# Gated delta rule on one core: both runs inverted at once in 64-row halves, and a shorter table of constants

## The reference

```python
gam = jnp.cumsum(gc, axis=-1)
incl = jnp.tril(jnp.ones((CHUNK, CHUNK), bool))
strict = jnp.tril(jnp.ones((CHUNK, CHUNK), bool), -1)
decay = jnp.exp(jnp.where(incl, gam[..., :, None] - gam[..., None, :], -jnp.inf))
kk = jnp.einsum("bhnld,bhnsd->bhnls", kc, kc)
a_mat = jnp.where(strict, bc[..., :, None] * kk * decay, 0.0) + jnp.eye(CHUNK, dtype=q.dtype)
rhs = jnp.concatenate([vc * bc[..., None], kc * (bc * jnp.exp(gam))[..., None]], axis=-1)
sol = lax.linalg.triangular_solve(a_mat, rhs, left_side=True, lower=True, unit_diagonal=True)
u, w = sol[..., :dv], sol[..., dv:]
qk = jnp.einsum("bhnld,bhnsd->bhnls", qc, kc) * decay
q_dec = qc * jnp.exp(gam)[..., None]
k_dec = kc * jnp.exp(gam[..., -1:] - gam)[..., None]
...
    v_new = u_i - jnp.einsum("bhld,bhdv->bhlv", w_i, state)
    o_i = jnp.einsum("bhld,bhdv->bhlv", qd_i, state) + jnp.einsum("bhls,bhsv->bhlv", qk_i, v_new)
    state = cd_i[..., None, None] * state + jnp.einsum("bhld,bhlv->bhdv", kd_i, v_new)
```

## Time and profile before

| | |
|---|---|
| time, median of 3 runs | 3710.27 us (3708.34 to 3712.47) |
| the profiled execution | 3719.07 us, its span 3716.9 us |
| mean granted TensorE clock of the span | 0.919 |
| busy: PE, DVE, ACT, POOL | 3155.8, 1509.2, 884.0, 310.2 us |
| gd_chunks | 2275.97 to 2402.96 us of the span |

### The profile page before, as it was taken

The page is one execution under the profiler, slowest core; times in us unless marked ns, Lnnn a source line. Parts: engine busy times, 40 slices in busy tenths (PEclk is TensorE's granted clock), DMA queues, the critical chain, the costliest instruction groups (busy, mean ns, idle before and its releaser), DMA issues. The chain is left out here.

```text
span 3716.9 us, 94167 instructions
## 1 busy us (share of the span) xinstructions
PE 3155.8 (85%) x41870; PEld 2282.9 (61%) x41870; DVE 1509.2 (41%) x2497; ACT 884.0 (24%) x1486; POOL 310.2 (8%) x259
## 2 busy tenths in 40 slices
PE   4978879998787788886997947775899999999996
PEld 2855467887464666674886936733466666666653
DVE  3353653333653554546565875535111111111111
ACT  2113323222222343331453532201011111010110
POOL 0020200000311122230000014200000000000000
PEclk6988899999897999998998968987899999999998
DMA  5253432222033100103653510030999999999993
GB/s 199 80 161 123 152 135 102 91 101 103 34 129 143 49 21 28 42 4 125 227 198 117 187 64 1 28 140 28 350 405 405 406 406 406 406 407 406 405 406 146
DMA packets 220145, 684.74 MB, mean 184 GB/s; under 512 B 25776, under 2 KB 50608, under 8 KB 187008
## 3 DMA queue, kind: packets, MB, share of 16 engines
q1 hardware_dynamic: 190144, 648.49, 45.7%
q10 hardware_dynamic: 29760, 32.69, 2.6%
HBM read 660.15 MB, written 20.97 MB: 183 GB/s over the span
## 5 line engine op out<-in xcount | busy, mean ns | idle before, releaser
L3358 PE MATMUL experts_psum_gu<-ring,experts_x 128*32 128x256 f32 x9216 | 508.6, 381 | 16.4 <-ACT experts_x L3402 16.4
L3358 PEld LDWEIGHTS experts_psum_gu<-ring,experts_x 128*32 128x32 f32 x9216 | 294.9, 110 | 220.9 <-ACT experts_x L3402 16.9
L3462 DVE TENSOR_TENSOR experts_gate<-experts_psum_gu,experts_bias 128x768 f32<-128x768 f32 x32 | 30.6, 958 | 864.6 <-PE experts_psum_gu L3358 864.6
L3381 PE MATMUL experts_psum_down<-experts_weights,experts_hiddenT 128*32 128x256 f32 x6144 | 338.8, 380 | 3.8 <-ACT experts_hiddenT L3410 3.8
L3381 PEld LDWEIGHTS experts_psum_down<-experts_weights,experts_hiddenT 128*32 128x32 f32 x6144 | 199.4, 110 | 137.3 <-issue 5.5
L811 PE MATMUL mlp_psum_bank<-mlp_x_high,mlp_w_high 128*128 128x512 f32 (+1 forms) x512 | 175.7, 343 | 12.5 <-DVE xT_rounded L328 12.5
L302 DVE TENSOR_TENSOR ring_rounded<-ring,mlp_w_high 128x1024 fp32r<-128x1024 f32 x128 | 156.7, 1226 | 51.0 <-ACT mlp_w_high L297 51.0
L811 PE MATMUL mlp_psum_bank<-xT_rounded,mlp_w_high 128*128 128x512 f32 (+1 forms) x512 | 173.8, 339 | 0.0
L3406 ACT ACTIVATE experts_sigmoid<-experts_gate 128x768 f32<-128x768 f32 x32 | 27.0, 843 | 616.1 <-DVE experts_gate L3464 616.1
L811 PE MATMUL mlp_psum_bank<-mlp_x_high,ring_rounded 128*128 128x512 f32 (+1 forms) x512 | 173.2, 338 | 0.0
L3358 PE MATMUL experts_psum_gu<-xT,experts_x 128*32 128x256 f32 x3072 | 171.6, 379 | 0.0
(11 more groups left out here) (698 smaller groups left out, 5903.5 us busy)
## 6 DMA issues: line engine op xcount, KB each, us to landing
ring<-in_w_gu SPq DMA_DIRECT2D x186, 1024.0 KB, 19.0
experts_weights<-in_w_down SPq DMA_DIRECT2D x128, 1024.0 KB, 21.1
ring<-in_ada_w SPq DMA_DIRECT2D x36, 2048.0 KB, 9.2
ring<-in_mlp_w SPq DMA_DIRECT2D x32, 2048.0 KB, 8.8
xT<-in_w_gu SPq DMA_DIRECT2D x64, 1024.0 KB, 20.9
ring<-in_w_in SPq DMA_DIRECT2D x12, 2048.0 KB, 7.7
ring<-in_ab_w_in SPq DMA_DIRECT2D x6, 2048.0 KB, 10.3
ring<-in_w_rkv SPq DMA_DIRECT2D x6, 2048.0 KB, 8.3
```

The lines of the kernel that those rows point to most:

```text
L3358: mm = nc.tensor.matmul(pg[o, q, gr, :], x, w[:, c:c + C], start=(u == 0 and gr != 1), stop=(u == U - 1), skip_group_check=True)
L3381: mm = nc.tensor.matmul(pd[o, gr, :], hidT[:, ch, gr, GROUP * v:GROUP * v + GROUP], w[:, ch, C * c:C * c + C], start=(v == 0 and ch == 0 a ...
L3462: v.tensor_tensor(gt[:, :, :], pg[:, 0, 0:GROUPS, :], rep(bias[:, 0, :], GROUPS), ALU.add).then_inc(s_bg, 1)
```

## The change

- The inverse of a run is made of halves: L has only the diagonal 64x64 blocks of all eight heads of a run, the block below the diagonal goes to L21 (in og, which is free until the output). Six levels on quarters of the array invert the diagonal blocks, as in rw_chunks, but with the X correction in the last level too; banks and lanes now belong to the runs, so that both runs are inverted in the same rounds. Then two products join the halves: T = L21 Y (join), and X T (off). Yf is the whole inverse, put together by copies.
- The decays of all four cells (run, lane) come first. DVE takes one difference of 128x512, ACT makes two Relu and two Exp of it, POOL puts beta's sign and size into the mask (row_mask). DVE's operations by head become operations over four or eight heads, and ktok is scaled in one.
- Tails: run 0 is solved, then its state and output, then the state's products for run 1, then run 1. Two of DVE's copies go to ACT.
- The masks of the levels are cut from the table of rw_chunks by two DMAs of this stage; the table of constants keeps 6 of its 20 blocks. Class Inverse is gone.

```diff
-C_LVL = 6
-N_BLOCKS = 6 + 2 * LEVELS
+N_BLOCKS = 6
...
-    blocks += lower + [m.T for m in lower]
...
-def gd_chunks(g, feat, ktok, vtok, beta, ga, cums, og):
...
-        inv = Inverse(g, ph)
...
+        decT, rhs = ([[spare[:, 4 * q + 2 * i + l, :, :] for l in range(2)] for i in range(2)] for q in range(2))
+        dead = feat[:, 16:32, :].rearrange("p (q a) (b c) -> p q (a b) c", q=8, b=2)
+        wide, dif, decL, rowmask = ([dead[:, 2 * q + l, :, :] for l in range(2)] for q in range(4))
+        Yf = [g.x[:, i, :].rearrange("p (h c) -> p h c", h=M8) for i in range(2)]
+        L21 = [og[:, i, 512:1024].rearrange("p (h c) -> p h c", h=M8) for i in range(2)]
...
+        masks = Fetch(g, "ldgdn", [(ident[:, :], table[:, C2_ID * CH:C2_ID * CH + CH]),
+                                   (levels[:, :, :].rearrange("p k c -> p (k c)"),
+                                    table[:, C2_LVL * CH:(C2_LVL + HALF_LEVELS) * CH])])
...
+        other = lambda m, c: cs(c if m % 2 == 0 else 1 - c)
+        place = lambda m: 4 * (1 - m % 2) + m // 2
+        T_of = lambda i, m: T[i][:, 4 * (m % 2) + m // 2, :]
+        Y_of = lambda i, m: Y[i][:, place(m), :]
+        t_bank = lambda i, m: banks[i][:, m % 2, 64 * (m // 2):64 * (m // 2) + 64]
+        y_bank = lambda i, m: banks[i][:, 1 - m % 2, 256 + 64 * (m // 2):320 + 64 * (m // 2)]
...
+                def differ(i, l):
+                    take(s_gb[l])
+                    if i:
+                        take(s_expT[l])
+                    v.tensor_tensor(dif[l], b4(l, 0), rep(cums[:, i, 4 * l:4 * l + 4], P, 2), ALU.subtract)\
+                        .then_inc(s_dif[l], 1)
+
+                def halves(i, l):
+                    take(s_mL[l])
+                    kk = b4(l, 1)
+                    for c in range(2):
+                        ch.mark(v.tensor_tensor(L[i][cs(c), 4 * l:4 * l + 4, :], kk[cs(c), :, cs(c)], decL[l][cs(c), :, cs(c)],
+                                                ALU.mult))
+                    ch.mark(v.tensor_tensor(L21[i][cs(1), 4 * l:4 * l + 4, :], kk[cs(1), :, cs(0)], decL[l][cs(1), :, cs(0)],
+                                            ALU.mult))
+                    ch.wait()
+                    v.sem_inc(s_L[l], 1)
...
+                def start(i):
+                    for l in range(2):
+                        take(s_L[l])
+                    v.tensor_tensor(Lo[i][:, :, :], L[i][:, :, :], rep(levels[:, 0, :], M8), ALU.mult).then_inc(s_l0[i], 1)
+                    take(s_l0[i])
+                    v.tensor_tensor(T[i][:, :, :], Lo[i][:, :, :], rep(ident[:, :], M8), ALU.add).then_inc(s_x0[i], 1)
...
+                    v.memset(Yf[i][cs(1), :, cs(0)], 0.0).then_inc(s_zero, 1)
+                masks.wait(dve)
+                for i, l in cells:
+                    halves(i, l)
+                    values(i, l)
+                    if (i, l) == (0, 1):
+                        differ(1, 0)
+                        differ(1, 1)
+                        start(0)
+                start(1)
+                ch.wait()
+                for l in range(2):
+                    v.sem_inc(s_rhs[l], 1)
+                for k in range(HALF_LEVELS):
+                    for i in range(2):
+                        take(s_yr[i])
+                        if k:
+                            v.tensor_tensor(pair(Y[i][:, :, :]), banks[i][:, 0:2, 256:512], pair(Y[i][:, :, :]), ALU.add)\
+                                .then_inc(s_yc[i], 1)
...
+                            take(s_xc[i])
+                            take.n[s_xc[i].name] += HALF_LEVELS - 1
+                            v.tensor_copy(pair(Y[i][:, :, :]), banks[i][:, 0:2, 256:512]).then_inc(s_yc[i], 1)
+                for i in range(2):
+                    take(s_yc[i], HALF_LEVELS)
+                    for c in range(2):
+                        v.tensor_copy(Yf[i][cs(c), :, cs(c)], Y[i][cs(c), :, :]).then_inc(s_full[i], 1)
+                for i in range(2):
+                    take(s_off[i])
+                    v.tensor_copy(Yf[i][cs(0), :, cs(1)].rearrange("p (q a) c -> p q a c", q=2),
+                                  banks[i][cs(0), 0:2, 256:512].rearrange("p q (a c) -> p q a c", c=CH)).then_inc(s_full[i], 1)
...
+                def row_mask(i, l):
+                    if i:
+                        take(s_mL[l])
+                    v.tensor_tensor(rowmask[l], strict, rep(nb[:, i, 4 * l:4 * l + 4], P, 2), ALU.mult).then_inc(s_row[l], 1)
...
+                for i, l in cells:
+                    take(s_expL[l])
+                    take(s_row[l])
+                    v.tensor_tensor(decL[l], decL[l], rowmask[l], ALU.mult).then_inc(s_mL[l], 1)
+                    take(s_expT[l])
+                    v.tensor_tensor(decT[i][l], decT[i][l], incl, ALU.mult).then_inc(s_mT[l], 1)
+                    if i == 0:
+                        row_mask(1, l)
...
+                for k in range(1, HALF_LEVELS):
+                    for i in range(2):
+                        take(s_yr[i] if k == 1 else s_t[i])
+                        v.tensor_tensor(Lo[i][:, :, :], L[i][:, :, :], rep(levels[:, k, :], M8), ALU.mult).then_inc(s_lo[i], 1)
...
+                def decays(i, l):
+                    take(s_dif[l])
+                    if i:
+                        take(s_L[l])
+                    nc.scalar.activation(decL[l], dif[l], ACT.Relu).then_inc(s_pos[l], 1)
+                    take(s_pos[l])
+                    nc.scalar.activation(decL[l], decL[l], ACT.Exp, scale=-1.0).then_inc(s_expL[l], 1)
+                    nc.scalar.activation(decT[i][l], dif[l], ACT.Relu, scale=-1.0).then_inc(s_neg[l], 1)
+                    take(s_neg[l])
+                    nc.scalar.activation(decT[i][l], decT[i][l], ACT.Exp, scale=-1.0).then_inc(s_expT[l], 1)
...
+                for k in range(1, HALF_LEVELS):
+                    for i in range(2):
+                        take(s_t[i])
+                        nc.scalar.copy(pair(T[i][:, :, :]), banks[i][:, 0:2, 0:256]).then_inc(s_tc[i], 1)
+                    for i in range(2):
+                        take(s_xr[i])
+                        nc.scalar.copy(X[i][:, :, :], banks[i][:, 2, :].rearrange("p (m c) -> p m c", m=M8)).then_inc(s_xc[i], 1)
+                for i in range(2):
+                    take(s_join[i])
+                    for q in range(2):
+                        nc.scalar.copy(T[i][cs(q), 4 * q:4 * q + 4, :],
+                                       banks[i][cs(q), q, 0:256].rearrange("p (a c) -> p a c", c=CH)).then_inc(s_joinc[i], 1)
...
+                def level_t(i):
+                    take(s_lo[i])
+                    take(s_yc[i])
+                    for m in range(M8):
+                        for c in range(2):
+                            mm = nc.tensor.matmul(t_bank(i, m)[other(m, c), :], Lo[i][cs(c), m, :], Y_of(i, m)[cs(c), :],
+                                                  start=True, stop=True)
+                    mm.then_inc(s_t[i], 1)
+
+                def level_yx(k, i):
+                    take(s_tc[i])
+                    take(s_xc[i])
+                    for m in range(M8):
+                        for c in range(2):
+                            mm = nc.tensor.matmul(y_bank(i, m)[cs(c), :], X[i][other(m, c), m, :], T_of(i, m)[other(m, c), :],
+                                                  start=True, stop=True)
+                    mm.then_inc(s_yr[i], 1)
+                    if k == 1:
+                        for c in range(2):
+                            nc.tensor.matmul(banks[i][cs(c), 2, :], ident[cs(c), :],
+                                             X[i][cs(c), :, :].rearrange("p a b -> p (a b)"), start=True, stop=False,
+                                             skip_group_check=True)
+                    for m in range(M8):
+                        for c in range(2):
+                            mm = nc.tensor.matmul(banks[i][other(m, c), 2, m * CH:m * CH + CH], T_of(i, m)[other(m, c), :],
+                                                  X[i][other(m, c), m, :], start=False, stop=(k == HALF_LEVELS - 1),
+                                                  skip_group_check=True)
+                    mm.then_inc(s_xr[i], 1)
+
+                def join(i):
+                    take(s_yc[i])
+                    for m in range(M8):
+                        mm = nc.tensor.matmul(t_bank(i, m)[other(m, 0), :], L21[i][cs(1), m, :], Y_of(i, m)[cs(1), :],
+                                              start=True, stop=True)
+                    mm.then_inc(s_join[i], 1)
...
+                def off(i):
+                    take(s_joinc[i], 2)
+                    take(s_xc[i])
+                    for m in range(M8):
+                        mm = nc.tensor.matmul(y_bank(i, m)[cs(0), :], X[i][other(m, 0), m, :], T_of(i, m)[other(m, 0), :],
+                                              start=True, stop=True)
+                    mm.then_inc(s_off[i], 1)
...
+                for i, l in cells:
```

(27 more changed lines are left out.)

367 lines of the change are left out of this document (147 added, 220 removed).

## The result

| | before | after |
|---|---|---|
| time, median (4 runs each) | 3711.37 us (3708.34 to 3713.83) | 3669.51 us (3668.51 to 3672.71) |
| ratio | | 0.989, 95% interval 0.9878 to 0.9903 |
| the profiled execution, its span | 3719.07, 3716.9 us | 3672.71, 3670.9 us |
| gd_chunks | 127.0 us | 83.3 us |
| the first norm starts at | 51.24 us | 50.67 us |

The change makes the program 1.1% faster, 41.9 us. The forecast was 3656.7, 53.6 us faster, and its range ended at 3669.0; the result lies just above it. The direction and the order of size were right, the size was not.

A forecast was written before the change was run, and what follows sets the result against it. gd_chunks was taken as unoverlapped, its preparations led by VectorE and its inverses bound by TensorE. Gains of 14.5 (preparations), 36.3 (inverses), 0.4 (tails) and 2.4 (table) sum to 53.6, from 3710.3 to 3656.7 us; range 3647 to 3669.

The forecast's parts named there:

- Preparations: Start of gd_chunks: all four cells prepared in one go, 40.5 us before, about 26 after, gain 14.5.
- The bounds of this term, 22 to 33: Preparation: 22 us if no operations collide, 33 if all collide and 64x256 pieces cost 0.68 each.
- The rival of the long preparation: Preparation and inverse: all collisions, dearer halves or more TensorE pauses, 4 to 12 us more, 3661 to 3669; chance 0.20.
- a sign of being wrong: Preparation: the forecast is wrong if GpSimd rather than VectorE is what it waits for.
- First level: Inverse, from its first pass to the first T product: 4.46 us, taken from rw_chunks, paid once.
- It fits: First level: the 4.46 us already holds a stretch at the slow clock after TensorE idles.
- Levels: Inverse: levels 1 to 4 at 22.9 us as in rw_chunks, level 5 with its X update at 4.96.
- Joining: End of the inverse: L21 products, copies, second product and waits, 4.0 us, hardly below 3 or above 6.
- tails: End of gd_chunks: solves, states and outputs, 13.9 us before, about 13.5 after, gain 0.4.
- The table: Program start: constants shrink from 20 blocks to 6, 0.918 MB less before the first norm, gain 2.4 us.
- The rival of no gain at the start: Program start: first norm waits for something other than the DMA queue, 2.4 us less gain, 3659; chance 0.05.
- the slower case: Inverse: quarter products do not overlap, five levels cost 86 us more, program at 3743 us; chance 0.02.

The follow-up runs named there:

- run 0: Not a follow-up experiment: the first of the two 128-token runs that gd_chunks processes, solved before the other.
- run 1: Not a follow-up experiment: the second of the two 128-token runs that gd_chunks processes; its right-hand side needs the first one's state.
- thin: Changed kernel with GpSimd's 12 preparation masks cut to 32 of 512 elements, result incomplete; preparation 27.63 us against 31.85, stage 79.0 us, one run without a ratio.
- warm: Changed kernel plus 36 and 32 unused whole-array products where TensorE idled in the preparation; stage 79.7 us against 83.3, ratio to the kernel before 0.9878.
- gamma: Changed kernel with run 1's decay rows in their own buffers and bank, all rows made first; preparation 25.25 us against 31.85, ratio to the kernel before 0.9863.
- late: Changed kernel with key and value scaling and the clearings moved from preparation into levels; preparation 27.51 us against 31.85, ratio to the kernel before 0.9869.
- early: both with preparation banks sorted by run, so run 0's first level starts during run 1's matrices; stage 72.9 us, ratio to the kernel before 0.9858.
- seq: Changed kernel inverting the two runs one after the other in the same halves; first product to first solve 48.50 us, stage 94.0, ratio to the kernel before 0.9919.
- both: Changed kernel with the edits of gamma and late together; preparation 20.74 us, stage 72.4 us, ratio to the kernel before 0.9847.
- bothwarm: both plus 20 unused whole-array products behind run 1's products; first level 3.24 us, stage 69.5 us, ratio to the kernel before 0.9852.
- c20b: Second run of the changed kernel with the constant table back at 20 blocks, 14 unused; stage 86.7 us, tail 15.04 us, no ratio.
- both2: The same kernel as both, run again; stage 73.1 us, tail 15.07 us, ratio to the kernel before 0.9857.

## Why the prediction missed

The profiled executions differ by 46.4 us, of which the stage makes 43.7 and the start 0.6; the rest, 2.1, arose in code that did not change; where was not followed. The medians differ by 41.9, with an interval of 36 to 45 us: the stage and the start lie inside it. The sum of 53.6 was too large by 9.3 for what the change did, and these are its terms.

- **Preparations, 26 forecast, 31.9 measured: the step that failed.** Its four parts: VectorE's own work without collisions 17.9, measured 18.6 (thin); collisions 3.4, measured 3.9; waits for TensorE beyond its own work 4.3, measured 8.2; waits for completion 0.4, about 1.1.

  So the sum of operations was nearly good (the pieces of 64x256 take 0.42 to 0.44 us and not 0.34: with a fixed part, half the elements cost more than half), and the wait was not: I took TensorE's 24 passes per head group as mostly hidden behind VectorE's work (4.3 of 10.7 us left), at the pace of the higher clock. Too little of them was hidden: 8.2 of TensorE's 13.2 busy us were waited for. VectorE has next to nothing to do beside run 0's products (0.7 us between its two differences), and run 1's products may not start before run 0's matrix has left their bank, and the first of them run at the lower clock (at the higher one, in warm, the third wait is gone). The order of the two engines in the excerpts above showed the first, the bank formulas in the code the second.

  gamma took this cause away, and 6.6 us went. thin shows that the rest of the preparation is nearly one chain on VectorE, as assumed, and late that part of what is taken out of it comes back as a wait for TensorE. The bounds of this term, 22 to 33, held the 31.9, but by luck: their upper end was made of collisions and dearer pieces, and the range took only +5 of it.

  The rival of the long preparation named the collisions, which were right, and TensorE's pauses, but not this wait; its range of 3661 to 3669 is still nearest to the result. GpSimd, named as a sign of being wrong, is not what the preparation waits for.
- **First level, 4.46 forecast, 5.02.** Taken from rw_chunks, where the granted clock is 0.66 in the mean of that stretch. Here TensorE had idled for 8.3 us and the whole of it ran at 0.50. "It fits" was wrong by 0.6; warm gives 3.24 at 1.00.
- **Levels, 27.9 forecast, 28.7.** Right, with 27.8 to 30.6 over the runs. Pauses for issue are 3.1 to 4.9 us of that, and in early the lower clock adds to it.
- **Joining, 4.0 forecast, 4.17; tails, 13.5 forecast, 13.6.** Right.
- **The table, 2.4 forecast, 0.6 in the profile and 0.8 over several.** The rival of no gain at the start was nearer. A DMA share of 1.03 says that the bytes before are all paid, not that all engines end together.
- **The rivals.** Quarter products overlap here as in rw_chunks (61 T passes take 1.10 us), so the slower case was rightly given little. X's 32 passes, which all write one bank and add to what lies there, take 1.09 us (2324.00 to 2325.09 in seq), and Y's 32, which alternate between two banks, 0.51. No run varied the banks, so why X is twice as slow is open. The Trainium skill (TensorEngine Tiling (Array Packing), Restrictions and Gotchas) says that different row tiles cannot use one PSUM bank at the same time. For T the trace does not agree, since its two halves write one bank at 61 passes in 1.10 us; for X no run here can tell.
- **From span to median.** Before's profiled execution was 8.8 us above its median, after's 3.2 above. I carried the 8.8 over to both. That is 5.6 us which no reading of the stage could have given, and it belonged in the range, as the spread of 14 us between the profiles' unchanged parts shows. Terms and this together: 9.3 - 2.1 + 5.6 = 12.8, the miss of the median.

A version that beats both kernels came of it: both and bothwarm, with ratios to before of 0.9847 and 0.9852, against 0.9892 for the changed kernel measured again; these ratios don't tell the two from each other. By the stage, which repeats better, they win 10.6 and 13.5 us over the change (83.0 to 72.4 and 69.5). Next to go would be GpSimd's masks, for which VectorE waits 1.7 us and with which it collides.

## What to carry to other kernels

When several sets of the same work are merged into one pass, list for each product whose bank or buffer it overwrites: a shared bank turns two sets into a chain, and its price here was the other engine's whole time, part of it at the lower clock. Price what an engine waits for by walking the order of both engines, not by the sum of its own work. And work that nobody awaits belongs behind the first point at which the engine would idle anyway: late was a move of lines and brought 4.3 us.

## What the runs showed beside that

- The granted clock fell in the tail in three profiles (late, c20b, both2): 0.89, 0.90 and 0.90 in the mean, and the tail took 15.0 to 15.2 us instead of 13.6, with TensorE busy 14.3 to 14.4 of them. In the eleven other profiles with the same tail it was 1.00. It is one stretch at the lower level, 0.50, at the start of the tail, and 1.00 after it. The joining just ahead keeps TensorE busy 2.7 of 4.2 us, but it does so in the other eleven too; what decides was not found. In late, from where the clock fell:

```profile
2344.70:2348.10 3.40, 3.40 (x19) 3.40 (x18) 0.00 (x0) 0.84 (x2) 0.00 (x0) 0.50 0.02 5
2348.10:2359.51 11.41, 10.68 (x95) 10.49 (x94) 6.47 (x19) 3.25 (x6) 0.00 (x0) 1.00 0.00 0
```

- Hiding a piece of work can cost as much as it saves where it leaves a hole behind: early split TensorE's first level in two with 3.9 us of idling between, and the products behind the hole ran at the lower clock for 9 us.
- Unused products in TensorE's idle time cost nothing here: the 68 of warm and the 20 of bothwarm lengthened no stretch of the stage, and shortened the first level by 1.8 and 1.2 us.
